# Complex power tables of a state-space mixer: from VectorE to GpSimd, with GpSimd's other instructions cut in half

## The chip, the core and the metric

One core of a Trainium2 chip runs the whole program. The metric is device time in microseconds. The engines are named as in the profile: PE is TensorE, DVE is VectorE, ACT is ScalarE, POOL is GpSimd, SP issues most transfers.

## The reference

The program computes a two-layer trunk over 512 tokens of width 1024 in float32. What matters here is the first half-step feed-forward and the state-space mixer (S5) behind it:

```python
x = x + 0.5 * swiglu(rms_norm(x, g[0]), ffn_w_in[l, 0], ffn_w_out[l, 0])
h = rms_norm(x, g[1])
# S5: 64 groups of 16 channels, 64 complex states each
lam_bar = jnp.exp(lam * step)                       # one complex number per state
b_bar = ((lam_bar - 1.0) / lam)[..., None] * b
# x_t = lam_bar x_{t-1} + b_bar u_t ;  y_t = Re(C x_t) + D u_t
```

The kernel computes the recurrence in 64 steps of 8 tokens. For that it needs powers of `lam_bar` times B and C (the block operators), and tables of the real and imaginary part of the phase after each of the 64 steps. Both depend on the weights alone, and they are made while the first feed-forward runs on PE.

## The kernel before

**The weights.** The feed-forward is computed to nearly float32 precision from packs of 128x1024 weights. SP loads pack n into one of four slots of `w_raw` (L475) once DVE has split pack n-4. ACT copies it rounded into `w_split` (L749) once PE has used up pack n-4, DVE subtracts to get the remainder (L1159, the DVE instruction `split`), and PE multiplies three times for each tile (L1590, L1591, L1592). One pack takes PE 24 matmuls.

**The first feed-forward** runs as two halves, `FFN0A1` (packs 0 to 32) and `FFN0A2` (33 to 65), each of 11 tiles of the inner dimension. The IN part has two packs a tile, and behind it the gate: DVE L1169, ACT L755, DVE L1171, ACT L757, DVE L1173 (`g_split`). The OUT part has 11 packs, for eight output tiles d = 0 to 7 of eleven products each; DVE adds each tile to the stream `x_res` (L1259, L1260). The first output tile needs all 11 gated tiles, the last one too.

**The block operators.** There are eight blocks of eight groups. `make_powers(k)` on POOL makes `CP` and `BP` with six TENSOR_TENSOR instructions (L569, L574, L576 of 1152 elements a partition; L579, L580, L582 of 1024), signals `s_made`, and stores part of `CP` with a transfer of its own. PE then turns block k (`turn_block`, L1663 and L1667) at a fixed place of its own order, written in `TURN_AT`: block 0 after IN tile 4, blocks 1 and 2 after IN tiles 7 and 9, blocks 3 and 4 after OUT tiles 2 and 5, blocks 5 to 7 after IN tiles 2, 5 and 8 of the second half. PE waits there for `s_made`. `make_powers(k)` in turn waits at L574 until PE has turned block k-1. ACT and DVE finish the block (`copy_ops`, `block_taps`) at the places in `TAPS_AT`, and SP stores it.

**The tables.** `block_tables(k)` on DVE (L1202 to L1208) makes the phase tables of block k: four products into `gate`, `up` and the two halves of a part of `OUTB`, and then a subtraction and an addition. The factors are `PA` and `PB`, where neighbouring powers of one group lie 64 elements apart; one factor of each product is repeated along the innermost dimension, and the other is read with steps of 64 elements. The places in `TABLES_AT` say after which tile DVE does so, and from the same places `table_stores` works out behind which weight pack SP waits for the tables (`s_phase`) and stores them. Block k's tables may overwrite `OUTB` once those of block k-1 are stored (`s_tabst`).

**POOL's order**: preparations, `make_powers(0)`, powers for `PB`, `make_powers(1)`, powers of `PB`, `make_powers(2)`, powers of `PA`, a memset that signals `s_near`, then `make_powers(3)` to `(7)`, then the loads of finished operators.

Of the kernel before, what the change touches and what calls it, by code (L numbers as in the profile page):

```python
# [28 lines left out]
ALU = mybir.AluOpType  # L29
# [3 lines left out]
P = 128  # L33
# [24 lines left out]
FFN0A1 = 0  # L58
FFN0A2 = FFN0A1 + 3 * HALF
# [14 lines left out]
TILES = {FFN0A1: HALF, FFN0A2: HALF, FFN0B: FT, FFN1A: FT, FFN1B: FT}  # L74
F_BASE = {FFN0A1: 0, FFN0A2: HALF, FFN0B: FT, FFN1A: 2 * FT, FFN1B: 3 * FT}
# [5 lines left out]
IN, OUT = range(2)  # L81
# [2 lines left out]
           (FFN0A2, IN, 2): 5, (FFN0A2, IN, 5): 6, (FFN0A2, IN, 8): 7}  # L84
TAPS_AT = {(FFN0A1, IN, 5): 0, (FFN0A1, IN, 8): 1, (FFN0A1, IN, 10): 2, (FFN0A1, OUT, 3): 3, (FFN0A1, OUT, 6): 4,
           (FFN0A2, IN, 3): 5, (FFN0A2, IN, 6): 6, (FFN0A2, IN, 9): 7}
TABLES_AT = {(FFN0A1, OUT, 0): 0, (FFN0A1, OUT, 1): 1, (FFN0A1, OUT, 4): 2, (FFN0A2, IN, 1): 3, (FFN0A2, IN, 4): 4,
             (FFN0A2, IN, 6): 5, (FFN0A2, IN, 8): 6, (FFN0A2, IN, 10): 7}

N_IN0A, N_S5, N_IN0B, N_KV, N_LAT, N_DQ, N_IN1B, N_FINAL = range(8)  # L90

# [14 lines left out]
O_B, O_COS, O_SIN, O_C, O_T = 0, 1024, 1536, 2048, 3072  # L106
# [3 lines left out]
def build(nc, xT, wstream, cols, consts, mask, pos, lam, bcd, dskip, out):  # L110
# [18 lines left out]
    GT = at("gate", [P, SEQ], F32, o_s + 2 * K)  # L129
    UT = at("up", [P, SEQ], F32, o_s + 4 * K)  # L130
# [27 lines left out]
    PW = tmp("lam_pow", [P, 2, M, GROUPS])  # L158
    PWS = tmp("lam_pow_signed", [P, 2, M, GROUPS])
    PA = tmp("u64_pow", [P, 2, 8, GROUPS])  # L160
    PB = tmp("u8_pow", [P, 2, 8, GROUPS])
    EC = tmp("e_coef", [P, 2, GROUPS])
    BC = [tmp("bc_in_even", [P, 4, GB * GC]), at("bc_in_odd", [P, 4, GB * GC], F32, o_s + 16 * K)]
    CP = tmp("c_pow", [P, GB, M, GC])
    BP = tmp("b_pow", [P, GB, T, GC])
    OUTB = tmp("ops_out", [P, 2048])
    DS = tmp("d_skip", [GC, GROUPS])
    DI = tmp("d_eye", [GC, GB, GC])
    TM = tmp("s5_tmp", [P, GB * M * GC])
# [39 lines left out]
    def sem(name):  # L209
        return nc.alloc_semaphore(name)  # L210
# [8 lines left out]
    s_tabst = sem("tables_stored")  # L219
# [15 lines left out]
    s_g_hi, s_g_lo = sem("g_hi"), sem("g_lo")  # L235
# [6 lines left out]
    s_cp = sem("c_and_b_steps")  # L242
    s_phase, s_window = sem("phase_steps"), sem("taps_in_window")
    s_small = sem("coefficients_ready")
    s_zero_taps = sem("taps_before_zero")
    s_near, s_sq0, s_sum0 = sem("table_powers_ready"), sem("first_squares"), sem("first_squares_added")
    s_ang, s_rope, s_pch = sem("rope_angles_reduced"), sem("rope_tables_ready"), sem("pool_step")

    s_made, s_turned, s_taps, s_btc = sem("powers_made"), sem("ops_turned"), sem("taps_ready"), sem("b_op_copied")
# [28 lines left out]
    def block_groups(k):  # L278

        return slice(k * GB, (k + 1) * GB)  # L280
# [132 lines left out]
    with nc.Block() as block:  # L413
# [115 lines left out]
        def _(pool):  # L529
# [8 lines left out]
            tt, ts = nc.gpsimd.tensor_tensor, nc.gpsimd.tensor_scalar  # L538
# [10 lines left out]
            def make_powers(k):  # L549

                first = k == 0

                def chan(ap):
                    return ap.rearrange("p (g c) -> p g c", g=GB)

                def power(tab, ri, n):
                    return (tab[:, ri, 0:n, block_groups(k)].rearrange("p m g -> p g m").unsqueeze(3)
                            .broadcast_to([P, GB, n, GC]))

                def spread(ap, n):  # L560
                    return chan(ap).unsqueeze(2).broadcast_to([P, GB, n, GC])

                tmc = TM[:].rearrange("p (g m c) -> p g m c", g=GB, m=M)
                tmb = TM[:, 0:GB * T * GC].rearrange("p (g m c) -> p g m c", g=GB, m=T)
                if k + 1 < BLOCKS:
                    pool.dma_start(BC[(k + 1) % 2][:], bcd[k + 1]).then_inc(s_bc[(k + 1) % 2], 16)
                bc = BC[k % 2]
                pool.wait_ge(s_bc[k % 2], 16 * (k // 2 + 1))
                tt(tmc, spread(bc[:, 3, :], M), power(PWS, 1, M), ALU.mult)  # L569
                if not first:  # L570

                    pool.wait_ge(s_turned, k)
                    pool.wait_ge(s_cpst, k * 16)
                tt(CP[:], spread(bc[:, 2, :], M), power(PWS, 0, M), ALU.mult).then_inc(s_cp, 1)  # L574
                pool.wait_ge(s_cp, k * 3 + 1)
                tt(CP[:], CP[:], tmc, ALU.subtract).then_inc(s_cp, 1)  # L576

                pool.wait_ge(s_cp, k * 3 + 2)
                tt(BP[:], spread(bc[:, 0, :], T), power(PW, 0, T), ALU.mult)  # L579
                tt(tmb, spread(bc[:, 1, :], T), power(PW, 1, T), ALU.mult).then_inc(s_cp, 1)  # L580
                pool.wait_ge(s_cp, k * 3 + 3)
                tt(BP[:], BP[:], tmb, ALU.subtract).then_inc(s_made, 1)  # L582
                pool.wait_ge(s_made, k + 1)
                pool.dma_start(ops_dram[k][:, O_C:O_T].rearrange("p (g n) -> p g n", g=GB),
                               CP[:, :, 1:M, :].rearrange("p g m c -> p g (m c)")).then_inc(s_cpst, 16)


            nc.gpsimd.memset(RSTD[:], 0.0).then_inc(s_warm, 1)
# [49 lines left out]
            make_powers(2)  # L638
            squared(tt, link, (PA[:, 0, 1, :], PA[:, 1, 1, :]), (PB[:, 0, 4, :], PB[:, 1, 4, :]), t1, t2)
            powers(tt, link, PA, 7, t1, t2)  # L640
            nc.gpsimd.memset(TM[:, 0:8], 0.0).then_inc(s_near, 1)
            pool.wait_ge(s_near, 1)
            for k in range(3, BLOCKS):
                make_powers(k)


            pool.wait_ge(s_opdma, 16 * OPS_STORES * BLOCKS)
# [492 lines left out]
        def _(dve):  # L1140
# [8 lines left out]
            tt, ts, stt = nc.vector.tensor_tensor, nc.vector.tensor_scalar, nc.vector.scalar_tensor_tensor  # L1149
# [34 lines left out]
                link(ts(dst[:], bank[:], 1.0 / width, EPS, ALU.mult, ALU.add))  # L1184
                nc.vector.reciprocal(dst[:], dst[:]).then_inc(s_rcp, 1)

            def block_tables(k, F):

                if k == 0:
                    dve.wait_ge(s_near, 1)  # L1190
                else:

                    dve.wait_ge(s_tabst, k * 16)
                dve.wait_ge(s_g_lo, F + 1)
                gs = block_groups(k)
                ar, ai = (PA[:, ri, :, gs].rearrange("p a g -> p g a").unsqueeze(3).broadcast_to([P, GB, 8, 8])
                          for ri in range(2))
                br, bi = (PB[:, ri, :, gs].rearrange("p b g -> p g b").unsqueeze(2).broadcast_to([P, GB, 8, 8])
                          for ri in range(2))
                ct, st, v1, v2 = (ap.rearrange("p (g a b) -> p g a b", g=GB, a=8) for ap in (  # L1200
                    OUTB[:, O_COS:O_COS + 512], OUTB[:, O_SIN:O_SIN + 512], GT[:], UT[:]))
                tt(v1, ai, bi, ALU.mult)  # L1202
                tt(v2, ar, bi, ALU.mult)
                tt(ct, ar, br, ALU.mult)
                tt(st, ai, br, ALU.mult).then_inc(s_phase, 1)
                dve.wait_ge(s_phase, k * 2 + 1)
                tt(ct, ct, v1, ALU.subtract)
                tt(st, st, v2, ALU.add).then_inc(s_phase, 1)  # L1208
                dve.wait_ge(s_phase, k * 2 + 2)

            def block_taps(k):

                link(tt(DI[:], DS[:, block_groups(k)].unsqueeze(2).broadcast_to([GC, GB, GC]),
# [901 lines left out]
```

## Time and profile before

| | |
|---|---|
| median of 3 runs | 1799.36 us (1798.47 to 1799.75) |
| the profiled execution: its own time | 1796.3 us |
| the profiled execution: its span | 1794.5 us |
| TensorE's mean granted clock | 0.997 |
| PE busy | 1773.4 us, 99% |
| DVE busy | 920.9 us, 51% |
| ACT busy | 646.2 us, 36% |
| POOL busy | 319.7 us, 18% |

The span goes from the first to the last instruction; the execution's own time is 1.8 us more. Busy shares are averages over the whole program: POOL is busy nearly all of its first 220 us, and hardly afterwards.

### The profile page before, as it was taken

How to read it: one execution, taken by the hardware profiler on the slowest of the kernel's cores; microseconds unless marked ns; L12 is line 12 of the kernel's file. 1: busy time of each engine (PE TensorE's matmuls, PEld its weight loads, DVE VectorE, ACT ScalarE, POOL GpSimd, SP SyncE). 2: the span in 40 equal slices, each digit the busy share in tenths (PEclk: the TensorE clock that was granted, in tenths of full speed). 3: DMA queues.
4: the chain of work that ended last, by engine and by line, in shares of the span. 5: the costliest groups of instructions: out<-in, count | busy, mean ns of one | idle time of the engine just before them, and what ended most of it. 6: DMA issues, size and time to landing. Idle time of an engine off the chain costs nothing.

```text
span 1794.5 us, 21493 instructions
## 1 busy us (share of the span) xinstructions
PE 1773.4 (99%) x8142; PEld 1453.2 (81%) x8142; DVE 920.9 (51%) x1059; ACT 646.2 (36%) x884; POOL 319.7 (18%) x274
## 2 busy tenths in 40 slices
PE   9999899999999999999999999999999999999998
PEld 6887788879888888888888888888866888888887
DVE  7768978647555444433374444333664554444333
ACT  6342233347434333322253333222454433333222
POOL 8997533016014000000000000000100200000000
PEclk9999999999999999999999999999999999999999
DMA  5353635588422222222223222222310322222221
GB/s 199 118 171 117 185 132 167 160 311 295 136 99 94 94 95 103 95 94 95 103 74 116 94 94 100 99 94 94 123 36 1 106 106 100 99 94 94 98 91 47
DMA packets 80977, 207.24 MB, mean 115 GB/s; under 512 B 24048, under 2 KB 34416, under 8 KB 79888
## 3 DMA queue, kind: packets, MB, share of 16 engines
q1 hardware_dynamic: 69664, 189.86, 31.4%
q0 software_dynamic: 2784, 14.29, 2.4%
q10 hardware_dynamic: 8464, 2.20, 0.5%
q8 instruction: 44, 0.72, 0.2%
q14 instruction: 21, 0.17, 0.0%
HBM read 183.25 MB, written 23.07 MB: 115 GB/s over the span
## 4 chain that ended last, share of the span: by engine, by line
PE 90%; DVE 4%; POOL 3%; issue 2%; ACT 1%; DMA 1%; SPq 0%; ACTq 0%; DVEq 0%; POOLq 0%
PE bank L1590 28%; PE bank L1592 27%; PE bank L1591 27%; PE bank L1920 1%; DVE w_split L1159 1%; PE bank L1901 1%; PE bank L1903 1%; PE bank L1768 1%; PE bank L1785 1%; PE bank L1778 1%; ACT w_split L749 0%; PE bank L1912 0%; DVE ops_out L1208 0%; PE bank L1620 0%; DMA x_res<-xT 0%
## 5 line engine op out<-in xcount | busy, mean ns | idle before, releaser
L1159 DVE TENSOR_TENSOR w_split<-w_raw,w_split 128x1024 fp32r<-128x1024 f32 x296 | 399.3, 1353 | 624.8 <-ACT w_split L749 624.1
L1590 PE MATMUL bank<-h_split,w_split 128*128 128x512 f32 x1504 | 589.5, 392 | 2.3 <-DVE gate L1171 0.8
L1592 PE MATMUL bank<-h_split,w_split 128*128 128x512 f32 x1504 | 585.7, 389 | 0.0
L1591 PE MATMUL bank<-h_split,w_split 128*128 128x512 f32 x1504 | 585.6, 389 | 0.0
L749 ACT ACTIVATE w_split<-w_raw 128x1024 fp32r<-128x1024 f32 x296 | 312.1, 1058 | 639.3 <-PE bank L1592 631.4
L1590 PE MATMUL bank<-g_split,w_split 128*128 128x512 f32 (+1 forms) x854 | 330.2, 387 | 8.1 <-DVE w_split L1159 5.0
L1590 PEld LDWEIGHTS bank<-h_split,w_split 128*128 128x128 f32 x1504 | 282.4, 188 | 64.7 <-DVE h_split L1178 1.9
L1591 PEld LDWEIGHTS bank<-h_split,w_split 128*128 128x128 f32 x1504 | 282.5, 188 | 59.3 <-issue 1.4
L1592 PEld LDWEIGHTS bank<-h_split,w_split 128*128 128x128 f32 x1504 | 282.4, 188 | 58.6
L1591 PE MATMUL bank<-g_split,w_split 128*128 128x512 f32 (+1 forms) x854 | 329.5, 386 | 0.0
L1592 PE MATMUL bank<-g_split,w_split 128*128 128x512 f32 (+1 forms) x854 | 329.4, 386 | 0.0
L547 POOL TENSOR_TENSOR sq_sum<-sq_sum,sq 128x512 f32<-128x512 f32 x39 | 51.1, 1310 | 1063.7 <-ACT sq L768 1063.7
L1590 PEld LDWEIGHTS bank<-g_split,w_split 128*128 128x128 f32 x854 | 161.6, 189 | 40.7 <-DVE w_split L1159 5.4
L1592 PEld LDWEIGHTS bank<-g_split,w_split 128*128 128x128 f32 x854 | 161.5, 189 | 32.1
L1591 PEld LDWEIGHTS bank<-g_split,w_split 128*128 128x128 f32 x854 | 161.6, 189 | 31.7
L755 ACT ACTIVATE gate<-gate 128x512 f32<-128x512 f32 x88 | 55.6, 632 | 203.8 <-DVE gate L1169 203.7
L1173 DVE TENSOR_TENSOR g_split<-gate,g_split 128x512 f32 (+1 forms) x88 | 76.9, 874 | 80.7 <-ACT g_split L757 80.7
L1171 DVE TENSOR_TENSOR gate<-gate,bank 128x512 f32<-128x512 f32 x88 | 60.6, 688 | 62.7 <-ACT gate L755 62.7
L757 ACT ACTIVATE g_split<-gate 128x512 f32 (+1 forms) x88 | 55.6, 632 | 72.7 <-DVE gate L1171 72.7
L1169 DVE TENSOR_TENSOR gate<-bank,rstd 128x512 f32<-128x512 f32 x88 | 60.1, 683 | 1.4 <-ACT rstd L786 1.4
L761 ACT ACTIVATE h_split<-x_res,cols 128x512 fp32r<-128x512 f32 x48 | 33.0, 717 | 51.8 <-DVE x_res L1260 48.2
L768 ACT ACTIVATE sq<-x_res 128x512 f32<-128x512 f32 x41 | 25.6, 623 | 50.3 <-DVE x_res L1260 38.2
(283 smaller groups left out, 1163.8 us busy)
## 6 DMA issues: line engine op xcount, KB each, us to landing
w_raw<-wstream SPq DMA_DIRECT2D x296, 512.0 KB, 3.5
op_slot<-s_ops SPq DMA_DIRECT2D x5, 2048.0 KB, 11.3
s_ops<-ops_out SPq DMA_DIRECT2D x16, 512.0 KB, 2.9
op_slot<-s_ops POOLq DMA_DIRECT2D x3, 2048.0 KB, 14.2
s_ops<-c_pow POOLq DMA_DIRECT2D x8, 512.0 KB, 4.6
s_ops<-k_window SPq DMA_DIRECT2D x64, 64.0 KB, 3.4
x_res<-xT SPq DMA_DIRECT2D x8, 256.0 KB, 6.5
s_u<-x_gained ACTq DMA_DIRECT2D x8, 256.0 KB, 6.9
```

What stands on the lines that cost most here:

```text
L547: nc.gpsimd.tensor_tensor(ACC[:], ACC[:], SQ[:, k % 2, :], ALU.add).then_inc(s_sum, 1)
L749: nc.scalar.activation(W[:, r, 0, :], RAW[:, r, :], ACT.Copy).then_inc(s_hi, 1)
L755: nc.scalar.activation(GT[:], GT[:], ACT.Silu).then_inc(s_silu, 1)
L757: nc.scalar.activation(gt_part(f, 0), GT[:], ACT.Copy).then_inc(s_g_hi, 1)
L761: nc.scalar.activation(dst[:, k, 0, :], X[:, k, :], ACT.Identity, scale=col(gains + k)).then_inc(s_h_hi, 1)
L1159: tt(W[:, r, 1, :], RAW[:, r, :], W[:, r, 0, :].bitcast(F32), ALU.subtract).then_inc(s_lo, 1)
L1169: tt(GT[:], gb[:], RSTD[:], ALU.mult).then_inc(s_gate, 1)
L1171: tt(GT[:], GT[:], ub[:], ALU.mult).then_inc(s_read, 1)
L1173: tt(gt_part(f, 1), GT[:], gt_part(f, 0).bitcast(F32), ALU.subtract).then_inc(s_g_lo, 1)
L1590: mm(bank, hi, x_hi, start=start, stop=True, skip_group_check=True)
L1591: mm(bank, hi, x_lo, start=False, stop=True, skip_group_check=True)
L1592: return mm(bank, lo, x_hi, start=False, stop=True, skip_group_check=True)
```

## The change

`make_powers` writes each of its six instructions as two, over groups 0 to 3 and 4 to 7 of the block. `block_tables` is deleted from DVE, and the same six instructions, not in halves, stand in POOL's `make_tables`, with `TM` (POOL's scratch) in place of `gate` and `up`. `make_tables(0)` stands ahead of `make_powers(3)`, and the others are set between the later powers. `TABLES_AT`, which now only places SP's stores, is partly moved: the stores of tables 0 to 7 stand behind packs 30, 34, 39, 45, 49, 53, 59 and 63; before, they stood behind 31, 32, 36, 45, 51, 55, 59 and 63. `TURN_AT` and `TAPS_AT` stay.

```diff
-TABLES_AT = {(FFN0A1, OUT, 0): 0, (FFN0A1, OUT, 1): 1, (FFN0A1, OUT, 4): 2, (FFN0A2, IN, 1): 3, (FFN0A2, IN, 4): 4,
-             (FFN0A2, IN, 6): 5, (FFN0A2, IN, 8): 6, (FFN0A2, IN, 10): 7}
+TABLES_AT = {(FFN0A1, IN, 10): 0, (FFN0A1, OUT, 2): 1, (FFN0A1, OUT, 6): 2, (FFN0A2, IN, 1): 3, (FFN0A2, IN, 3): 4,
+             (FFN0A2, IN, 5): 5, (FFN0A2, IN, 8): 6, (FFN0A2, IN, 10): 7}
...
+                def in_halves(dst, a, b, op):
+                    for gs in (slice(0, GB // 2), slice(GB // 2, GB)):
+                        ins = tt(dst[:, gs], a[:, gs], b[:, gs], op)
+                    return ins
...
-                tt(tmc, spread(bc[:, 3, :], M), power(PWS, 1, M), ALU.mult)
+                in_halves(tmc, spread(bc[:, 3, :], M), power(PWS, 1, M), ALU.mult)
...
+            def make_tables(k):
+                if k >= 1:
+                    pool.wait_ge(s_tabst, k * 16)
+                gs = block_groups(k)
+                ar, ai = (PA[:, ri, :, gs].rearrange("p a g -> p g a").unsqueeze(3).broadcast_to([P, GB, 8, 8])
+                          for ri in range(2))
+                br, bi = (PB[:, ri, :, gs].rearrange("p b g -> p g b").unsqueeze(2).broadcast_to([P, GB, 8, 8])
+                          for ri in range(2))
+                ct, st, v1, v2 = (ap.rearrange("p (g a b) -> p g a b", g=GB, a=8) for ap in (
+                    OUTB[:, O_COS:O_COS + 512], OUTB[:, O_SIN:O_SIN + 512], TM[:, 0:512], TM[:, 512:1024]))
+                tt(v1, ai, bi, ALU.mult)
+                tt(v2, ar, bi, ALU.mult)
+                tt(ct, ar, br, ALU.mult)
+                tt(st, ai, br, ALU.mult).then_inc(s_phase, 1)
+                pool.wait_ge(s_phase, k * 2 + 1)
+                tt(ct, ct, v1, ALU.subtract)
+                tt(st, st, v2, ALU.add).then_inc(s_phase, 1)
+                pool.wait_ge(s_phase, k * 2 + 2)
...
-            nc.gpsimd.memset(TM[:, 0:8], 0.0).then_inc(s_near, 1)
-            pool.wait_ge(s_near, 1)
-            for k in range(3, BLOCKS):
-                make_powers(k)
+            make_tables(0)
+            make_powers(3)
+            make_tables(1)
+            make_powers(4)
+            make_tables(2)
+            make_powers(5)
+            make_tables(3)
+            make_tables(4)
+            make_powers(6)
+            make_tables(5)
+            make_powers(7)
+            make_tables(6)
+            make_tables(7)
...
-            def block_tables(k, F):
...
-                if (stage, place, i) in TABLES_AT:
-                    block_tables(TABLES_AT[stage, place, i], F)
```

## Rows read from the trace of the kernel before

**Rows 1.** The page, part 1: busy time, share of the span, instructions.

```profile
PE 1773.4 (99%) x8142; PEld 1453.2 (81%) x8142; DVE 920.9 (51%) x1059; ACT 646.2 (36%) x884; POOL 319.7 (18%) x274
```

**Rows 2.** Waits of PE, 0 to 420 us: total us, times, longest us.

```profile
PE bank L1590 <- DVE w_split L1159: 5.0, 1, 5.0
PE bank L1590 <- DVE g_split L1173: 3.2, 1, 3.2
...
PE bank L1590 <- DVE gate L1171: 0.8, 1, 0.8
...
PE bank L1663 <- POOL b_pow L582: 0.5, 1, 0.5
```

**Rows 3.** Windows: busy by engine (instructions), granted clock, DMA share, GB/s.

```profile
148.00:149.00 1.00, 1.00 (x4) 0.81 (x3) 1.00 (x1) 0.00 (x0) 0.92 (x2) 0.50 0.00 0
...
196.00:355.00 159.00, 158.19 (x766) 130.00 (x759) 121.44 (x111) 52.32 (x75) 49.69 (x22) 1.00 0.51 153
```

**Rows 4.** Timeline of PE: start us, us, instruction, idle before it.

```profile
142.89 0.39 PE L1592 MATMUL bank<-g_split,w_split 128*128 128x512 f32 x1
146.44 0.50 PE L1590 MATMUL bank<-g_split,w_split 128*128 128x512 f32 x1 [3.16 <-DVE g_split L1173]
...
163.90 0.63 PE L1663 MATMUL bank<-c_pow,b_pow 128*16 128x128 f32 x16
...
186.18 0.79 PE L1590 MATMUL bank<-g_split,w_split 128*128 128x512 f32 x1 [4.95 <-DVE w_split L1159]
...
191.84 0.40 PE L1591 MATMUL bank<-g_split,w_split 128*128 128x512 f32 x1
...
195.80 0.63 PE L1663 MATMUL bank<-c_pow,b_pow 128*16 128x128 f32 x16
```

**Rows 5.** Timeline of DVE, 97 to 188 us.

```profile
97.03 1.28 DVE L1159 TENSOR_TENSOR w_split<-w_raw,w_split 128x1024 fp32r<-128x1024 f32 x1
...
143.89 2.50 DVE L1173 TENSOR_TENSOR g_split<-gate,g_split 128x512 fp32r<-128x512 f32 x1 [0.70 <-ACT g_split L757]
...
167.15 2.26 DVE L1202 TENSOR_TENSOR gate<-u_pow 128x512 f32<-128x512 f32 x1 [0.85 <-DMA s_ops<-ops_out]
...
182.15 5.11 DVE L1159 TENSOR_TENSOR w_split<-w_raw,w_split 128x1024 fp32r<-128x1024 f32 x2
```

**Rows 6.** Timeline of POOL.

```profile
63.83 2.40 POOL L582 TENSOR_TENSOR b_pow<-b_pow,s_tmp 128x1024 f32<-128x1024 f32 x1
...
97.30 1.32 POOL L376 TENSOR_TENSOR u_pow<-u_pow,s_tmp 128x128 f32<-128x128 f32 x1
...
133.95 0.59 POOL L377 TENSOR_TENSOR u_pow<-u_pow,s_tmp 128x192 f32<-128x192 f32 x1
...
148.34 3.25 POOL L582 TENSOR_TENSOR b_pow<-b_pow,s_tmp 128x1024 f32<-128x1024 f32 x1
...
246.75 2.30 POOL L574 TENSOR_TENSOR c_pow<-bc_in_even,lam_pow_signed 128x1152 f32<-128x1152 f32 x1 [30.14 <-PE bank L1667]
```

**Rows 7.** POOL by line: duration ns min/median/max, first and last start.

```profile
L569 POOL TENSOR_TENSOR s_tmp<-bc_in_odd,lam_pow_signed x4: 2252/2270/2275, 75.8 to 261.2; 128x1152 f32<-128x1152 f32 x4
...
L582 POOL TENSOR_TENSOR b_pow<-b_pow,s_tmp x8: 2396/2958/3262, 63.8 to 292.6; 128x1024 f32<-128x1024 f32 x8
...
L547 POOL TENSOR_TENSOR sq_sum<-sq_sum,sq x12: 1282/1294/1332, 361.0 to 544.2; 128x512 f32<-128x512 f32 x12
```

**Rows 8.** POOL's small instructions, grouped by form: busy us, mean ns.

```profile
L375 POOL TENSOR_TENSOR u_pow<-u_pow 128x192 f32<-128x192 f32 x2 | 1.2, 596 | 0.0
...
L375 POOL TENSOR_TENSOR u_pow<-u_pow 128x64 f32<-128x64 f32 x3 | 1.0, 317 | 0.0
```

**Rows 9.** DVE's table instructions by line: duration ns min/median/max.

```profile
L1203 DVE TENSOR_TENSOR up<-u_pow x8: 1103/1117/3610, 159.2 to 346.9; 128x512 f32<-128x512 f32 x8
...
L1208 DVE TENSOR_TENSOR ops_out<-ops_out,up x8: 677/686/3165, 163.0 to 350.8; 128x512 f32<-128x512 f32 x8
```

**Rows 10.** Waits of SP's queue, 0 to 420 us.

```profile
SPq L444 <- DVE ops_out L1208: 52.4, 7, 16.6
```

More of the change, by code:

```diff
@@ L245, in build @@
     s_zero_taps = sem("taps_before_zero")
-    s_near, s_sq0, s_sum0 = sem("table_powers_ready"), sem("first_squares"), sem("first_squares_added")
+    s_sq0, s_sum0 = sem("first_squares"), sem("first_squares_added")
     s_ang, s_rope, s_pch = sem("rope_angles_reduced"), sem("rope_tables_ready"), sem("pool_step")
@@ L573, in make_powers @@
                     pool.wait_ge(s_cpst, k * 16)
-                tt(CP[:], spread(bc[:, 2, :], M), power(PWS, 0, M), ALU.mult).then_inc(s_cp, 1)
+                in_halves(CP, spread(bc[:, 2, :], M), power(PWS, 0, M), ALU.mult).then_inc(s_cp, 1)
                 pool.wait_ge(s_cp, k * 3 + 1)
-                tt(CP[:], CP[:], tmc, ALU.subtract).then_inc(s_cp, 1)
+                in_halves(CP, CP, tmc, ALU.subtract).then_inc(s_cp, 1)
                 pool.wait_ge(s_cp, k * 3 + 2)
-                tt(BP[:], spread(bc[:, 0, :], T), power(PW, 0, T), ALU.mult)
-                tt(tmb, spread(bc[:, 1, :], T), power(PW, 1, T), ALU.mult).then_inc(s_cp, 1)
+                in_halves(BP, spread(bc[:, 0, :], T), power(PW, 0, T), ALU.mult)
+                in_halves(tmb, spread(bc[:, 1, :], T), power(PW, 1, T), ALU.mult).then_inc(s_cp, 1)
                 pool.wait_ge(s_cp, k * 3 + 3)
-                tt(BP[:], BP[:], tmb, ALU.subtract).then_inc(s_made, 1)
+                in_halves(BP, BP, tmb, ALU.subtract).then_inc(s_made, 1)
                 pool.wait_ge(s_made, k + 1)
@@ L1185, in mean_rcp @@
                 nc.vector.reciprocal(dst[:], dst[:]).then_inc(s_rcp, 1)
-            def block_tables(k, F):
[L1189 to L1209, printed above, removed]
             def block_taps(k):
@@ L1218, in s5_ops @@
             def s5_ops(stage, place, i):
-                F = F_BASE[stage] + (i if place == IN else TILES[stage] - 1)
                 if (stage, place, i) in TAPS_AT:
                     block_taps(TAPS_AT[stage, place, i])
-                if (stage, place, i) in TABLES_AT:
-                    block_tables(TABLES_AT[stage, place, i], F)
             def ffn_in_turn(stage, i):
```

## The prediction

> **What bounds the kernel now.** I read the page first: PE is busy 99% of the span [rows 1], so the kernel is one long line of matmuls and only what makes PE wait, or lowers its clock, can be won. The page says little about where that happens, so the second view is the table of PE's waits over the first 420 us, the part that the change touches. It has two waits that count, 5.0 us for a weight split on DVE and 3.2 us for a gated tile on DVE, and two small ones, 0.8 us and 0.5 us [rows 2]. Third, the timeline of PE places them: the first ends at 146.44, at the start of the OUT part; the second at 186.18 [rows 4]. Fourth, the windows: behind the first wait, at 148 us, the granted clock is 0.50, which is 1.2 GHz, while from 196 to 355 us it is 1.00, and PE is there busy 158.19 of 159 us [rows 3]. So each long wait is paid twice. A matmul at full clock is followed by the next after 0.227 us. The windows show the first fall from about 147.3 to 150.7, 3.4 us at half speed: 1.7 us lost. From 186.18 to 191.84 there are 13 matmuls, worth 2.95 us, in 5.66 us: 2.7 us lost [rows 4]. The sum to be had is 3.3 + 1.7 + 5.1 + 2.7 = 12.8 us, 0.7% of the time.
>
> Fifth, the timelines of DVE and POOL side by side say why DVE is late. POOL and DVE instructions that read two operands from SBUF don't overlap. The `g_split` at 143.89 takes 2.50 us, where its work is 0.69 us. The second set of tables occupies DVE from 167.15 to 182.15, 15 us, and the split that PE needs starts only then [rows 5]. Alone, a table product takes 1.10 us and a table sum 0.68 us [rows 9], so the set would be 5.8 us. The rest is waiting for POOL's instructions of 2.3 to 3 us. The other way round it costs POOL too: the DVE split at 97.03 (1.28 us, to 98.31) holds up a POOL instruction of 128 elements, which takes 1.32 instead of 0.46 us [rows 5, 6]. That is 0.87 us lost to POOL for each weight split, and in the same way some 0.46 us for each `g_split`.
>
> **The change part by part.** *Tables off DVE.* The second wait goes, with its clock loss: 7.8 us. DVE then has one split (1.2 us) and at times one sum in each pack of 5.44 us, so nothing on DVE is late next. *Halves.* DVE waits at most half as long for POOL. The `g_split` at 143.89 was due at 143.12, when PE ran out. Its chain had two such waits, of 2.3 and 1.8 us; in halves I count about half of each, leaving PE a wait of some 0.5 us and no fall of the clock: the 0.8 us and 0.5 us waits of rows 2 had none. That is 4.5 us. The 0.8 us wait at 292 us, behind a set of tables, goes too.
>
> So PE, left alone, would reach its turn of block 3 at 163.9 - 4.5 = 159.4 instead of 163.90, and that of block 4 24.1 us later (195.80 - 163.90 - 7.8). What waits there is POOL's work, so the sum is made on POOL.
>
> *What a half costs.* POOL's instructions of 64 and 192 elements take 317 and 596 ns [rows 8]: 2.2 ns an element and, less the 0.04 us by which neighbours overlap, a fixed 0.12 to 0.14 us. Six more instructions a block are 0.7 us. *What the DVE takes from it.* Undisturbed, a block is 0.6 (transfer issue) + 2 x 2.24 (L569's smallest) + 2.6 (L576, by L582's rate) + 2 x 2.0 (L579 and L580 at L569's rate) + 2.4 (L582's smallest) + 0.3 = 14.4 us [rows 7]. Block 0 took 16.7 us from 49.54 to 66.23, so 2.3 us went to DVE. In halves DVE is let in twice as often. Its work per pack is fixed by PE: a split a pack and a `g_split` every second one are 0.87 + 0.23 = 1.1 us in 5.44 us, which over block 0 is 3.4 us and more. So block 0 is ready 0.7 + 1.3 = 2.0 us later than 66.23, and PE, which already waits 0.5 us for it [rows 2], waits 2.5 us there. POOL has then block 1, block 2 and the small powers to do, and ends them before at 134.54 [rows 6]. Now it ends them at 134.54 + 3 x 0.7 + 2.0 = 138.6 us. The bounds of this: 136.6 if DVE takes no more than it does now, 139.5 if it takes all it can.
>
> *What a set of tables costs on POOL.* No POOL row has this reading. Lower bound: a product at the rate of L569, whose factors are also repeated, 2252 x 512 / 1152 = 1.0 us, and a sum like L547, 1.29 us: 4 x 1.0 + 2 x 1.29 = 6.6 us [rows 7]. Upper bound: L547's 1.29 us times the ratio that DVE shows between a product (1.10) and a sum (0.68): 2.09 us, and the set is 10.9 us [rows 7, 9]. I take the repeated form with the surcharge in us that DVE shows, 1.0 + 0.43 = 1.43 us: 4 x 1.43 + 2.58, 8.4 us with the gaps, because one factor is repeated and one is read in large steps. The Trainium skill (GPSIMD Engine Reference, Performance pitfalls for Q7 kernels) says that a GpSimd core that reads with steps of more than 8 bytes pays about half more for each element. By that rule a product at 1.29 us would become 1.94 us, the set 10.3 us, and the time 1805.3 us instead of 1801.5, an estimate; no row here shows such a reading on POOL.
>
> *The sum.* Set 0 stands ahead of block 3: 138.6 + 8.4 + 15.1 (a block in halves) + 5.0 (DVE's share over the 4.4 packs in which PE moves) = 167.1 us. PE arrives at 159.4 + 2.0 = 161.4 and waits 5.7 us: the new wait is as long as the one removed. Then 1.25 us for the transfer's issue, set 1 with 8.4, block 4 with 15.1, DVE's share 5.0: 196.9 us. PE arrives at 167.1 + 24.1 and 2 us of low clock = 193.2, waits 3.7 us, and turns block 4 at 197.0 instead of 195.80. Behind it the clock is low for about 1.7 us' worth, which this kernel did not have there. From then on POOL is ahead: block 5 is wanted at about 246 (POOL waits 30.14 us there now [rows 6]) and needs 197 + 1.3 + 8.4 + 20 = 227. The later sets go into such waits, and set 7 is stored at about 340, where it now is at 354. Sum: + 1.2 + 1.7 - 0.8 = + 2.1 us. The profiled execution has 1796.3 us; that is 1798.4 for it. The median of the runs lies 3.1 us above the profiled one, and carried to it this is 1801.5 us.
>
> *SP.* It waits for table 1 behind pack 34 until about 177. It waited 52.4 us for tables already, at most 16.6 us at once [rows 10], and PE had no wait for it: a load has some 12 us in hand. Store 0 moves behind pack 30 and its operator stores, lands at about 159, and set 1 starts after 168. Nothing for either. DVE's order loses 48 instructions, ACT's none.
>
> **The rivals.** (1) POOL keeps ahead: sets of 6.6 us, DVE's share as now (3.6 us a block with its set). Block 3 is ready at 136.6 + 6.6 + 15.1 + 3.6 = 161.9, a wait of 1.5 us, and block 4 at 188.4, a wait of 2.4 us. That is 7.4 + 0.8 = 8.2 us faster: 1791.2 us. For it: the repeated factor is cheap on POOL (L569). Against: all three terms must be at their lower bound. (2) The reading in large steps is dear on POOL as it is on DVE: 10.9 us a set, twice, is + 5.0, and DVE's full share another + 1: + 8 us, 1807.5 us. It decides from about 9.3 us a set on. For it: DVE's ratio of 1.6. Against: POOL spends 2.2 ns on an element anyway, where DVE spends half of that, and part of the reading may hide behind it. This is the one on the other side. The skill's rule on large steps, quoted above, speaks for this rival. (3) The stores in SP's queue hold up the weight packs, as soon as a set is later than the 12 us in hand: 5 us of wait and 2.7 us of clock more, 1809. Against: rows 10.
>
> **How the numbers follow.** Forecast 0.42, of which its own range is 1798 to 1805; rival 1 0.22; rival 2 0.28; rival 3 0.04; the rest, 0.04, is evenly spread. Bounds of no change are 0.2%, 3.6 us, about what a measurement of this kernel can tell. Faster: rival 1 and 0.02. Same: 0.34 of the forecast and 0.02. Slower: 0.08 of the forecast (block 3 late by another 2 us), rivals 2 and 3. The range goes from rival 1 to rival 2 with a little of what is beyond, 1791 to 1809.
>
> **What would show it.** In PE's waits the 5.0 and 3.2 us are gone; in their place stand waits of L1663 for POOL's `b_pow`: 2.5 us at about 68, 5 to 6 us at 162, 3 to 4 us at 193. POOL's set takes 8.4 us and 1.4 us a product; its halves of L569 take 1.2 us. If set 0 ends before 145 and no wait for `b_pow` is over 2 us, rival 1 holds. The forecast is wrong most easily in DVE's share of POOL's time, which enters five times, and in the product's price, which enters eight.

## The result and the profile after

The changed kernel has a median of 1801.51 us (1799.24 to 1803.3, 14 runs) beside 1797.91 us (1795.88 to 1799.75, 14 runs) for the kernel before on the same chip. The ratio is 1.0018, with a 95% interval of 1.0012 to 1.0025: 3.2 us slower by the ratio, 3.6 us by the medians, which is inside the 0.2% that the prediction calls no change, at its upper edge. The profiled execution has 1799.24 us, its span 1797.3 us; before it was 1796.3 and 1794.5. It is the fastest of the 14, 2.3 us below the median, so the waits below are not those of a typical one; the run changed_again has a second profile.

The page of the changed kernel, its first line and part 1, answers to [rows 1]:

```profile
span 1797.3 us, 21531 instructions
...
PE 1773.2 (99%) x8142; PEld 1454.1 (81%) x8142; DVE 868.4 (48%) x1011; ACT 646.8 (36%) x884; POOL 408.8 (23%) x369
```

DVE has 52 us less and POOL 89 us more. PE is busy as long as before and the span is 2.8 us longer, so the time must be in PE's waits. The waits of PE in the changed kernel, 0 to 420 us, answer to [rows 2]:

```profile
PE bank L1674 <- POOL b_pow L567: 10.1, 3, 3.9
PE bank L1601 <- DVE w_split L1316: 2.6, 2, 2.3
...
PE bank L1601 <- DVE g_split L1211: 0.7, 1, 0.7
PE bank L1601 <- DVE gate L1209: 0.2, 1, 0.2
```

The waits for DVE of [rows 2], 5.0, 3.2 and 0.8 us, are gone or small, and 10.1 us of waits for POOL's `b_pow` stand in their place. (The 2.3 us for L1316 is at 10 us, in a part that the change doesn't touch, and comes and goes with the execution.) PE's timeline of the changed kernel, with the idle time in brackets, places the three, and answers to [rows 4]:

```profile
69.36 1.05 PE L1674 MATMUL bank<-c_pow,b_pow 128*16 128x128 f32 x16 [2.35 <-POOL b_pow L567]
...
168.37 0.41 PE L1674 MATMUL bank<-c_pow,b_pow 128*16 128x128 f32 x4 [3.88 <-POOL b_pow L567]
...
197.81 0.28 PE L1674 MATMUL bank<-c_pow,b_pow 128*16 128x128 f32 x1 [3.89 <-POOL b_pow L567]
```

They are the turns of blocks 0, 3 and 4, the three places that the prediction named. The windows of the changed kernel (us, busy by engine, granted clock, DMA share, GB/s) answer to [rows 3]:

```profile
69.00:72.00 3.00, 2.64 (x25) 2.14 (x25) 2.30 (x3) 0.63 (x1) 2.60 (x7) 0.50 0.30 70
168.00:171.00 3.00, 2.63 (x25) 2.14 (x25) 0.00 (x0) 0.00 (x0) 2.68 (x4) 0.50 0.96 343
199.00:202.00 3.00, 3.00 (x11) 2.52 (x10) 0.00 (x0) 0.00 (x0) 2.98 (x4) 0.50 0.87 326
205.00:355.00 150.00, 150.00 (x712) 123.19 (x712) 93.69 (x75) 51.81 (x73) 110.59 (x73) 1.00 0.53 154
```

Behind each wait the granted clock is 0.50, 1.2 GHz. In finer windows it is low for 3.4 us each time, 1.7 us lost. The last row says where the change is good: from 205 to 355 us PE is busy all 150.00 us at 2.4 GHz, where it was 158.19 of 159 us before [rows 3]. The chain of waits, followed back from PE's turn at 197.81, is POOL without a gap from 34.81 us on, where the view begins: POOL is the bound from ahead of block 0 to block 4.

POOL's timeline of the changed kernel gives the dates (start, duration):

```profile
66.82 2.49 POOL L567 TENSOR_TENSOR b_pow<-b_pow,s_tmp 128x512 f32<-128x512 f32 x2
...
138.58 1.46 POOL L607 TENSOR_TENSOR s_tmp<-u_pow 128x512 f32<-128x512 f32 x1
...
164.85 3.46 POOL L567 TENSOR_TENSOR b_pow<-b_pow,s_tmp 128x512 f32<-128x512 f32 x2
...
194.42 3.34 POOL L567 TENSOR_TENSOR b_pow<-b_pow,s_tmp 128x512 f32<-128x512 f32 x2
```

Block 0 is ready at 69.3, set 0 begins at 138.58, block 3 is ready at 168.3 and block 4 at 197.8. The last product (L610) and the last sum (L613) of a set by line (min/median/max ns), which answer to [rows 9]:

```profile
L610 POOL TENSOR_TENSOR ops_out<-u_pow x8: 1454/1483/2464, 142.8 to 341.4; 128x512 f32<-128x512 f32 x8
...
L613 POOL TENSOR_TENSOR ops_out<-ops_out,s_tmp x8: 1282/1291/1302, 146.6 to 345.1; 128x512 f32<-128x512 f32 x8
```

SP's waits for tables, 52.4 us in [rows 10], are 3.6 us.

### The profile page after: what moved, and what is told of

Same layout as the page of the kernel before. It is cut to its first block, busy times and chain, and to the rows that moved or that the text cites. A ratio compares the mean times of both kernels' runs of the same rounds, so it can differ in the third digit from the quotient of the medians.

```text
span 1797.3 us, 21531 instructions
## 1 busy us (share of the span) xinstructions
PE 1773.2 (99%) x8142; PEld 1454.1 (81%) x8142; DVE 868.4 (48%) x1011; ACT 646.8 (36%) x884; POOL 408.8 (23%) x369
## 4 chain that ended last, share of the span: by engine, by line
PE 88%; POOL 10%; DVE 1%; issue 1%; ACT 1%; DMA 0%; SPq 0%; ACTq 0%; DVEq 0%; POOLq 0%
PE bank L1601 27%; PE bank L1602 27%; PE bank L1603 27%; POOL c_pow L567 2%; POOL s_tmp L567 2%; POOL b_pow L567 2%; PE bank L1931 1%; PE bank L1912 1%; PE bank L1914 1%; PE bank L1779 1%; PE bank L1796 1%; PE bank L1789 1%; POOL s_tmp L373 1%; POOL s_tmp L374 0%; PE bank L1923 0%
## 5 line engine op out<-in xcount | busy, mean ns | idle before, releaser
L1197 DVE TENSOR_TENSOR w_split<-w_raw,w_split 128x1024 fp32r<-128x1024 f32 x296 | 407.7, 1380 | 678.8 <-ACT w_split L787 678.4
L1211 DVE TENSOR_TENSOR g_split<-gate,g_split 128x512 f32 (+1 forms) x88 | 70.3, 799 | 80.7 <-ACT g_split L795 80.7
L1209 DVE TENSOR_TENSOR gate<-gate,bank 128x512 f32<-128x512 f32 x88 | 60.6, 688 | 62.6 <-ACT gate L793 62.6
```

Source lines behind the costliest of these rows:

```text
L1197: tt(W[:, r, 1, :], RAW[:, r, :], W[:, r, 0, :].bitcast(F32), ALU.subtract).then_inc(s_lo, 1)
L1209: tt(GT[:], GT[:], ub[:], ALU.mult).then_inc(s_read, 1)
L1211: tt(gt_part(f, 1), GT[:], gt_part(f, 0).bitcast(F32), ALU.subtract).then_inc(s_g_lo, 1)
```

## The experiments

Each series has its own runs of the kernel before, on the same chip: medians of 1796.48 us (series 1, 34 runs), 1796.10 us (series 2, 21), 1796.13 us (series 3, 22) and 1795.89 us (series 4, 9). All ratios are to these, with 95% intervals. The theory was the one of the prediction: PE waits for POOL because the sets stand ahead of blocks 3 and 4, and the halves take from POOL what they give to DVE. The main rivals were that the price of the sets decides, or what the halves do to PE's early waits. Each run lists the waits of one profiled execution, and its time is the median of all: in block0_whole, small_steps, powers_first_whole, powers_first_halves3 and spread_all_halves the profiled one lies 1.1 to 2.8 us above that median.

### Series 1: the two parts apart, and the order

**halves_alone**: the kernel before, with the halves at all powers; the tables stay on DVE.

```diff
+for gs in (slice(0, GB // 2), slice(GB // 2, GB)):
+    ins = tt(dst[:, gs], a[:, gs], b[:, gs], op)
```

> The kernel before with POOL's powers in halves and nothing else changed; the tables stay on DVE at their old places. Theory (POOL's blocks set PE's turns): block 0 is ready 2 to 3 us later, so PE waits about 2.4 us there and its clock falls for 3.4 us (1.7 us lost): +4. The wait of 3.2 us for g_split at the start of the OUT part shrinks to under 1 us with no fall of the clock: -4.5. The second set of tables on DVE takes some 11 instead of 15 us, so the split behind it is late by 1 us or less instead of 5: -6. Sum 4 to 8 us faster than before, near 1792 us. Rival (halves only cost POOL time and DVE gains nothing): the 5.0 us wait stays and the time is 2 to 4 us above before.

Measured: 1795.71 us, 0.9994 (0.9986 to 1.0003). Its waits of PE:

```profile
PE bank L1669 <- POOL b_pow L566: 5.2, 1, 5.2
PE bank L1596 <- DVE w_split L1165: 3.8, 3, 1.7
...
PE bank L1596 <- DVE g_split L1179: 1.1, 1, 1.1
```

A miss: 4 to 8 us were expected. The waits for DVE shrink as hoped (3.2 to 1.1 us, 5.0 to three of at most 1.7 us). But block 0 is ready at 71.1, 4.9 us later than at 66.2, and the wait of 5.2 us with 3.4 us of low clock behind it gives nearly all back. Of the 4.9 us the halves made 2.8: in this execution POOL began the block 2.1 us later too (51.63 instead of 49.54).

**tables_whole**: the changed kernel, with whole instructions.

```diff
-for gs in (slice(0, GB // 2), slice(GB // 2, GB)):
+for gs in (slice(0, GB),):
```

> The changed kernel with POOL's powers whole again; the tables stay on POOL and in the changed order. Theory: block 0 is back at 66 to 67 us with a wait of 0.5 us for it and no fall of the clock; set 0 begins at about 135 and takes 8.2 us; block 3 is ready at 160 to 161, where PE arrives at about 160; block 4 is ready at about 187, PE waits about 3 us. Sum about 6 to 8 us faster than before, 1790 to 1792 us. Rival (the tables on POOL cost the time, not the halves): waits for b_pow of 3 to 4 us at blocks 3 and 4 as in the changed kernel, and a time within 1 us of it.

Measured: 1799.09 us, 1.0012 (1.0003 to 1.002). A miss: slower instead of 6 to 8 us faster. By the ratios it is 1.1 us below the changed kernel, about what the rival had. The wait at block 3 is 0.64 us, but there is one of 9.39 us at block 4, with 10.2 us of low clock around it. POOL's timeline of this kernel shows half of the reason:

```profile
166.89 1.46 POOL L607 TENSOR_TENSOR s_tmp<-u_pow 128x512 f32<-128x512 f32 x1 [4.51 <-DMA s_ops<-ops_out]
```

POOL is done with block 3 at 161.1, and set 1 may not start, since set 0 is still in the buffer: SP issues its store at 160.74 only, behind the operator stores of block 2 (155.32 to 160.7). That is 4.5 of the 7.6 us by which block 4 is later than expected (194.65 instead of 187); in most of the rest, set 1 takes 10.8 us, disturbed by DVE, instead of 8.2. The store takes part as soon as POOL is fast; in the changed kernel POOL is late enough to hide it.

**powers_first_whole**: blocks 3 and 4 ahead of the sets, one set between, and the stores moved with them.

```diff
-order: T0 P3 T1 P4 T2 P5 T3 T4 P6 T5 P7 T6 T7, in halves
+order: P3 T0 P4 T1 T2 P5 T3 T4 P6 T5 P7 T6 T7, whole
-TABLES_AT = {(FFN0A1, IN, 10): 0, (FFN0A1, OUT, 2): 1, (FFN0A1, OUT, 6): 2, ...
+TABLES_AT = {(FFN0A1, OUT, 2): 0, (FFN0A1, OUT, 5): 1, (FFN0A1, OUT, 7): 2, ...
```

> The changed kernel with whole powers, and with POOL's order turned: block 3 ahead of set 0, block 4 ahead of set 1, and the stores of sets 0 to 2 at later places of SP's order. Theory: no wait of PE for b_pow but the 0.5 us at block 0. The wait of 3.2 us for g_split at the start of the OUT part comes back, with its fall of the clock (5 us), since block 3 runs there in whole instructions. Against before only the second wait (7.8 us) and the 0.8 us one are gone: 8 to 9 us faster, about 1789 us. Rival (POOL's total work counts, not its order): as the changed kernel.

Measured: 1793.76 us, 0.9983 (0.9975 to 0.9992), 2.7 us faster where 8 to 9 were expected. The waits at blocks 3 and 4 are gone. What remains: 2.21 us at block 0 with a fall of the clock, 1.54 us for ACT's operator copies at block 2, 1.94 us for a `g_split`, 2.00 us at 244.14 for the gate's product (DVE L1209) with another fall, 0.93 us at block 6.

**powers_first_halves3**: the same, with blocks 3 to 7 in halves.

```diff
-for gs in (slice(0, GB),):
+for gs in (slice(0, GB // 2), slice(GB // 2, GB)) if k >= 3 else (slice(0, GB),):
```

> As the kernel with the turned order, but with blocks 3 to 7 in halves and blocks 0 to 2 whole. Theory: the halves now stand only where PE doesn't wait for POOL, and the wait for g_split falls under 1 us without a fall of the clock: 12 to 13 us faster than before, about 1785 us. Rival (halves give nothing at g_split): equal to the kernel with the turned order and whole powers.

Measured: 1792.82 us, 0.9977 (0.9968 to 0.9986), 3.7 us faster where 12 to 13 were expected. The `g_split` wait falls to 0.65 us and the one at 244 is gone; one of 4.84 us, with 6.8 us of low clock, stands at block 6 (0.93 us in the run before). This execution is the slowest of the 11, 2.8 us above their median, so the others need not have it in this size. POOL's waits in this kernel, 200 to 300 us:

```profile
POOL s_tmp L607 <- DMA s_ops<-ops_out: 10.1, 2, 6.7
```

Two sets stand together there (T3, T4), and block 6 behind them: the second waits 3.39 us at 247.60 for the first to be stored. The order still puts work that PE awaits behind work that it doesn't.

### Series 2: block 0, the large steps, and a version without these faults

**block0_whole**: the changed kernel, with block 0 whole (`if k > 0` beside the halves).

> The changed kernel with block 0 alone whole again (blocks 1 to 7 in halves, sets on POOL, the changed order). Theory (POOL's chain up to block 4 sets the time): the wait at block 0 falls from 2.4 to 0.5 to 2.2 us, but what PE wins there it gives back at blocks 3 and 4, since POOL only gets the 0.7 us of split instructions and about 1 us of DVE's share back: block 4 at 195 to 196 us, time 1 to 2 us below the changed kernel (1799 to 1800 us by the median of the first series). Rival (the wait at block 0 with its fall of the clock is paid in full): 4 us below the changed kernel.

Measured: 1798.81 us, 1.0016 (1.0007 to 1.0025). The wait at block 0 is 0.55 us, but at block 3 it is 7.64 us and at block 4 3.81 us, 12.9 us in all with 0.86 us at block 2. What PE wins at block 0 it loses at block 3, where POOL sets the date: as the theory has it. The gain is smaller than the 1 to 2 us expected, since POOL has lost its lead again by block 4, which is ready at 198.1 and not at 195 to 196.

**small_steps**: the changed kernel, where the products read their second factor from neighbouring elements instead of in large steps. The tables then don't hold the phases.

```diff
-br, bi = (PB[:, ri, :, gs].rearrange("p b g -> p g b").unsqueeze(2)
+br, bi = (PB[:, ri].rearrange("p b g -> p (b g)")[:, 0:GB * 8].rearrange("p (g b) -> p g b", g=GB).unsqueeze(2)
```

> The changed kernel, with one part of the computation changed: POOL's four products of a set read their second factor from neighbouring elements of PB instead of elements 64 apart, so the tables don't hold the phases; everything else is the same, instruction for instruction. If the large steps have a price of their own, as the prediction took it, a product falls from 1.46 us to 1.05 to 1.1 us, a set from 8.1 to 6.5 us, block 3 is ready 1.6 us and block 4 3.2 us earlier, and the time falls by about 3 us. Rival (the price is that of any product with a repeated factor of 8 elements): a product stays at 1.46 us and the time too.

Measured: 1797.71 us, 1.0007 (0.9998 to 1.0016). The last product of this kernel, whose line number is one higher here:

```profile
L611 POOL TENSOR_TENSOR ops_out<-u_pow x8: 1154/1168/1623, 143.6 to 336.7; 128x512 f32<-128x512 f32 x8
```

The large steps cost 0.30 us of 1.46 us a product, 1.2 us a set: their price is shown. By the ratios the kernel is 2 us below the changed one, but the intervals of the two overlap. The waits for `b_pow` are 5.16, 3.45 and 3.40 us in its profiled execution, where block 0 was late (ready at 70.9), and blocks 3 and 4 are turned at 168.7 and 197.9, not earlier than in the changed kernel.

**dve_tables_halves3**: the kernel before, with only blocks 3 to 7 in halves and the tables on DVE; the guard `if k >= 3` as above.

> The kernel before, tables on DVE at their old places, with only blocks 3 to 7 in halves. Theory: block 0 is as before (wait 0.5 to 2.2 us), the 3.2 us wait for g_split falls to about 1 us, the 5.0 us wait behind set 1 to about 1 us as in the kernel with halves alone, and up to 3 us of short waits for weight splits stay in the second half: about 7 us faster than before, 1789 to 1790 us. Rival (halves alone had gained nothing because of DVE, not because of block 0): equal to halves alone, 1795 to 1796 us.

Measured: 1789.29 us (1788.9 to 1790.2, 5 runs), 0.9962 (0.9949 to 0.9976). As expected: halves are worth 6.8 us without a single table moved, if block 0 is left whole. What is left are three waits for weight splits, 3.7 us together, and 1.6 us for a `g_split`.

**sets_spread**: powers_first_halves3, with every set behind a block that PE awaits and no two sets together while a block is due soon.

```diff
-order: P3 T0 P4 T1 T2 P5 T3 T4 P6 T5 P7 T6 T7
+order: P3 T0 P4 T1 T2 P5 T3 P6 T4 P7 T5 T6 T7
-TABLES_AT = {..., (FFN0A2, IN, 1): 3, (FFN0A2, IN, 3): 4, (FFN0A2, IN, 5): 5, ...
+TABLES_AT = {..., (FFN0A2, IN, 1): 3, (FFN0A2, IN, 4): 4, (FFN0A2, IN, 7): 5, ...
```

> As the kernel with the turned order and blocks 3 to 7 in halves, and set 4 moved behind block 6 and set 5 behind block 7, with their stores later, so that no block waits behind two sets. Theory: the 4.8 us wait for block 6 and its fall of the clock, seen in one execution, go; no wait for b_pow remains but the one at block 0; 3 to 7 us below that execution, and by the medians 0 to 3 us below that kernel, 1790 to 1793 us. Rival (set 4 later holds up a store and with it SP's weight packs): a new wait for a weight split at 270 to 320 us, and no gain.

Measured: 1785.17 us (1785.01 to 1785.59, 5 runs), 0.9938 (0.9924 to 0.9952): 10.9 us below the kernel before, and more than the 1790 to 1793 us that were expected. By the ratios it is 7.0 us below powers_first_halves3. Its waits of PE, 0 to 420 us:

```profile
PE bank L1601 <- DVE g_split L1211: 1.8, 2, 1.5
PE bank L1601 <- DVE w_split L1316: 1.6, 1, 1.6
...
PE bank L1674 <- POOL b_pow L567: 0.5, 1, 0.5
```

Up to the end of this part the granted clock does not fall once. It is 4.1 us below dve_tables_halves3, which has the same halves, the tables on DVE and was measured beside it; no run of one reaches those of the other. So moving the tables to POOL is right; the changed kernel placed them wrongly.

### Series 3: what the halves are worth once the order is right

**spread_all_halves**: sets_spread, with all blocks in halves (no guard).

> The kernel with the sets spread out (the fastest so far, 1785.2 us), but with all eight blocks in halves instead of 3 to 7. Theory: nothing later absorbs the wait at block 0 here, so it is paid in full: block 0 is ready 3 to 5 us later, the clock falls behind it (1.7 us), and the time is 4 to 7 us above 1785. Rival (splitting block 0 costs no more than its 0.7 us, and the longer waits for it seen so far were scatter): within 1.5 us of 1785.

Measured: 1790.21 us, 0.9964 (0.9952 to 0.9977), 5.0 us more than sets_spread by the medians, 4.7 by the ratios. Blocks 1 and 2 are in halves here too, but no wait stands at them. Its waits have one new row, at block 0, with the clock low from 69.0 to 75.8:

```profile
PE bank L1674 <- POOL b_pow L567: 5.1, 1, 5.1
```

**spread_whole**: sets_spread, with no block in halves.

> The same kernel with no block in halves. If the halves are what shortens the wait at the start of the OUT part, it comes back at 3.2 us with a fall of the clock (1.7 us), and the time is 3 to 5 us above 1785. Rival (with the tables off DVE the whole instructions do as well): within 1.5 us of 1785.

Measured: 1795.6 us, 0.9996 (0.9987 to 1.0005), 10.4 us more than sets_spread where 3 to 5 were expected. Its waits:

```profile
PE bank L1601 <- DVE gate L1209: 5.8, 3, 3.5
PE bank L1601 <- DVE g_split L1211: 3.2, 2, 3.0
```

The longest of the `gate` waits, 3.49 us, ends at 301.19. DVE's timeline of this kernel there:

```profile
289.33 9.82 DVE L1197 TENSOR_TENSOR w_split<-w_raw,w_split 128x1024 fp32r<-128x1024 f32 x2
```

and POOL's:

```profile
289.15 0.93 POOL L591 DMA_DIRECT2D s_ops<-c_pow  x1 [0.30 <-POOL b_pow L567]
290.10 1.48 POOL L607 TENSOR_TENSOR s_tmp<-u_pow 128x512 f32<-128x512 f32 x1
291.52 1.47 POOL L608 TENSOR_TENSOR s_tmp<-u_pow 128x512 f32<-128x512 f32 x1
292.95 1.46 POOL L609 TENSOR_TENSOR ops_out<-u_pow 128x512 f32<-128x512 f32 x1
294.38 1.46 POOL L610 TENSOR_TENSOR ops_out<-u_pow 128x512 f32<-128x512 f32 x1
295.92 2.15 POOL L612 TENSOR_TENSOR ops_out<-ops_out,s_tmp 128x512 f32<-128x512 f32 x1
```

Two splits whose work is 2.4 us take 9.82 us, of which the first takes 7.59, while four products of POOL each run at their undisturbed 1.46 us: none let DVE in. The sum at L612, before which POOL waits for its own products, is the first that takes longer (2.15 instead of 1.29 us). That gave a new theory: DVE gets in where POOL waits for a semaphore, not reliably between instructions that follow one another.

**changed_again**: the changed kernel, unchanged.

> The changed kernel itself, on one chip with the two others. The first series gave 1.0018 of before. By the theory it is 14 to 17 us above the kernel with the sets spread out, with waits for b_pow at blocks 0, 3 and 4 of 8 to 14 us together in its profile and low clock behind at least two of them.

Measured: 1800.02 us, 1.002 (1.0011 to 1.0029). The waits for `b_pow` are 3.91 us at 69.61, 3.90 at 168.75 and 3.72 at 198.17. The wait at block 0, 2.35 us in the first profile, is 3.91 us here. The time is 14.9 us above sets_spread and the waits are 11.5 us together, with low clock behind each: as expected.

### Series 4: the new theory

**spread_whole_waits**: spread_whole, with a wait of POOL behind each of the first three products of a set. No instruction is cut.

```diff
-tt(v1, ai, bi, ALU.mult)
-tt(v2, ar, bi, ALU.mult)
-tt(ct, ar, br, ALU.mult)
+link(tt(v1, ai, bi, ALU.mult))
+link(tt(v2, ar, bi, ALU.mult))
+link(tt(ct, ar, br, ALU.mult))
```

> The kernel with the sets spread out and whole powers (1795.6 us, 10 us above its twin with blocks 3 to 7 in halves), with one edit: POOL waits for each of the first three products of a set before it starts the next. In its trace a weight split of DVE took 7.6 us, from 289.33 to 296.92, while POOL ran four products one behind the other, each in its undisturbed 1.46 us. If DVE isn't let in between POOL instructions that follow without a wait, the waits open three more gaps a set: no split takes more than some 3.5 us beside a set, PE's waits for the gate at 240 us (2.0 us) and 301 us (3.5 us, with a fall of the clock) go, and the time falls by 5 to 8 us, to 1788 to 1791. A set takes 0.2 us more alone. Rival (what counts is the length of the single instruction, and the whole powers cause the 10 us): products are held up nowhere new and the time stays within 1.5 us of 1795.6.

Measured: 1789.47 us, 0.9965 (0.9951 to 0.9979): 6.1 us less than spread_whole (each against 1796.13 or 1795.89 us before). The same place in POOL's timeline of this kernel:

```profile
292.77 1.47 POOL L608 TENSOR_TENSOR s_tmp<-u_pow 128x512 f32<-128x512 f32 x1
294.32 1.80 POOL L609 TENSOR_TENSOR ops_out<-u_pow 128x512 f32<-128x512 f32 x1
296.20 2.35 POOL L610 TENSOR_TENSOR ops_out<-u_pow 128x512 f32<-128x512 f32 x1
```

and DVE's:

```profile
293.74 1.06 DVE L1211 TENSOR_TENSOR g_split<-gate,g_split 128x512 fp32r<-128x512 f32 x1 [0.70 <-ACT g_split L795]
294.72 2.49 DVE L1197 TENSOR_TENSOR w_split<-w_raw,w_split 128x1024 fp32r<-128x1024 f32 x1
```

Now the products take turns with DVE (1.80 and 2.35 us), and from 200 to 355 us the longest split takes 3.70 us instead of 7.59. The `gate` waits are gone. A `g_split` wait of 2.99 us at 147.92, beside the powers and with low clock behind it, and 2.2 us at block 0 remain.

The traces bear the theory out beyond this place. In all 14 together, 53 weight splits of the first 360 us take over 3.8 us. In each of them the last 1.2 us, which is what a split alone takes, begin where POOL comes to a semaphore wait. In spread_whole two of them are beside sets, in spread_whole_waits none. Such a split costs time only where PE has nothing in hand: sets_spread, the fastest kernel, has four of them, of 5.6 to 7.6 us.

## Why the prediction was right in its total, and where its steps failed

The way to the time held: two waits for DVE go, three for POOL come, and the sum is about nothing. That 1801.5 us was forecast and 1801.51 measured is luck. The forecast is + 2.1 us on a median of 1799.36 us from 3 runs of the kernel before. Over 14 runs this median is 1797.91, 1.45 us lower, and the change adds 3.6 us (3.2 by the ratio), 1.5 us more.

- **Tables off DVE**, -7.8 us: the wait at 186 us is gone, and that at 292 us.
- **Halves**, -4.5 us: right in size, for another reason. PE's wait for `g_split` at the start of the OUT part is 0.74 us (expected 0.5), with no fall of the clock. But POOL runs set 0 beside it here (138.6 to 147.9), which is not in halves, where the kernel before runs block 3. In tables_whole, with no halves at all, the wait is 1.28 us and the clock doesn't fall either. So most of this term came from the order, and about 0.5 us from the halves.
- **Set 0's start**, 138.6 us: 138.58, which is in part luck: the 2.0 us in this sum hold the 0.7 us of block 0's split instructions, which 3 x 0.7 counts again, and POOL began block 0 0.7 us later than before. **The product**, 1.43 us: 1.46; the set of 8.4 us takes 9.3 us (set 0, to 147.9, with 1.0 us of DVE's share) and 8.3 us (set 1, undisturbed). **A block in halves with DVE's share**, 15.1 + 5.0 = 20.1 us: 20.1 (block 3) and 19.5 (block 4), from the issue of its transfer.
- **Block 3**, ready at 167.1: 168.3. The wait is 3.88 us instead of 5.7, since PE comes at 164.5 and not at 161.4. Of these 3.1 us, 1.7 are the low clock behind block 0, which the sum left out; 1.2 us PE was late already when it came to block 0 (67.0 us; before 65.8), most likely by the 2.3 us wait at the start of this execution, behind which the clock is low for 3.4 us.
- **Block 4**, turned at 197.0 with 3.7 us of wait: 197.81 and 3.89, and the clock falls behind it as said. Of the 1.2 us by which block 3 was late, 0.8 are left. The profiled execution has 1799.24 us instead of 1798.4, the same 0.8 us more.
- **Behind block 4** POOL is ahead, PE has no wait: right, 150.00 of 150 us. The last set is stored only at about 356 us, as before, not at 340: set 7 waits 8.56 us for the store of set 6, and POOL's loads of the finished operators wait 9.89 us for the store of set 7. It costs nothing: PE has no wait from 205 to 420 us.
- **Rival 1** (POOL keeps ahead) is out: set 0 ends at 147.9. **Rival 3** is out: SP's waits for tables fell to 3.6 us.
- **Rival 2** had the direction: large steps cost something, but not the set of 10.9 us. Without the large steps a product takes 1.17 us, with them 1.46: 25% more. The Trainium skill (GPSIMD Engine Reference, Performance pitfalls for Q7 kernels) has half more for an element read in large steps. Here one of the two factors is read so; where the rule and the measurement differ, the measurement decides. From the rule the prediction estimated a product of 1.94 us and a time of 1805.3 us.

Three steps failed, though the sum did not show it, because their errors lay where something else set the date.

*"In halves, DVE waits at most half as long for POOL"* fails. The size of POOL's instruction is not all that DVE waits for. In the changed kernel a split starts at 148.40, while POOL still issues a transfer, and takes 6.30 us, beside four halves of 128x576 elements of which none is disturbed. DVE's timeline of the changed kernel:

```profile
148.40 6.30 DVE L1197 TENSOR_TENSOR w_split<-w_raw,w_split 128x1024 fp32r<-128x1024 f32 x1
```

and POOL's:

```profile
148.85 2.42 POOL L567 TENSOR_TENSOR s_tmp<-bc_in_odd,lam_pow_signed 128x576 f32<-128x576 f32 x2
151.21 2.40 POOL L567 TENSOR_TENSOR c_pow<-bc_in_odd,lam_pow_signed 128x576 f32<-128x576 f32 x2
153.69 3.74 POOL L567 TENSOR_TENSOR c_pow<-c_pow,s_tmp 128x576 f32<-128x576 f32 x2
```

Its work of 1.2 us ends at 154.70, so it got in at about 153.5, at POOL's wait ahead of 153.69. At the same place in tables_whole, beside whole instructions, DVE's timeline has nearly the same:

```profile
144.47 6.05 DVE L1197 TENSOR_TENSOR w_split<-w_raw,w_split 128x1024 fp32r<-128x1024 f32 x1
```

Halves helped as a whole (dve_tables_halves3, -6.8 us), so cuts do let DVE in at times; series 4 shows that waits do it where instructions alone didn't. What decides between two halves without a wait was not found.

*"Block 0 is ready 2.0 us later"* is mis-sized. From the issue of its first transfer the block takes 16.5 to 16.7 us in all nine profiles in which it is whole, and 19.1 to 20.1 us in the five in which it is in halves: 2.4 to 3.4 us more. In halves it is ready at 69.3 to 71.1 us, 3.1 to 4.9 us later than before; the rest of that is POOL's start of the block, which lies between 49.5 and 51.6 us from one execution to the next, whole or in halves. And the wait has a fall of the clock behind it, which the sum left out. In a right order the halves of blocks 0 to 2 cost 5.0 us (spread_all_halves), with one wait, at block 0. In the changed kernel it is worth less: by the ratios (1.0018 and 1.002 beside block0_whole's 1.0016) 0.4 to 0.7 us, within the intervals nothing, because POOL is the bound at block 3 anyhow.

*"Nothing for either"*, said of SP, is right for this kernel only because POOL is late: the prediction had 9 us between the landing of store 0 at 159 and the start of set 1 at 168, and an earlier POOL uses them up. In tables_whole the store of set 0 costs POOL 4.51 us, and in powers_first_halves3 that of set 3 costs 3.39 us. Two misses of series 1 come in part from this edge.

Where did the expected gain go? Of the 12.8 us that the prediction counted as to be had, sets_spread gets 10.9, so they were there for the same parts in another order. They are not the sum of two independent parts. Blocks 3 to 7 in halves alone are worth 6.8 us (dve_tables_halves3, 0.9962). The tables on POOL in the good order, with whole powers, are worth nothing clear of noise (spread_whole, 0.9996): the wait at 186 us is gone, but POOL's sets now hold DVE up, and 5.8 us of waits for the gate stand in its place. Both together give 10.9 us. So the 7.8 us that the prediction gave to the tables alone show only if something lets DVE in. Between the changed kernel (1.0018 and 1.002) and sets_spread (0.9938) lie some 14.5 us. Of these, 5.0 us are the halves of blocks 0 to 2. The rest, 9.5 us, is the order, with the store places that belong to it; no run parts these two. The two waits of 3.9 us and their low clock in the changed kernel are of that size, 7.8 + 2 x 1.7 = 11.2 us.

## What to carry to other kernels

When work moves to the idle engine, it is its place in that engine's order that decides: first what the bound engine awaits, then the optional work, and no two pieces together that share a buffer if the store between them is slow. Where two engines hold each other up, let the other one in by waits in a long run of instructions, or by cutting them, but only in runs for which the bound engine doesn't wait itself. A sum that comes out right doesn't prove its terms: three of this one's were wrong in size or reason, and only kernels with another order, or with one part alone, showed it.

## What the hardware showed that was not expected

- DVE can be held over several POOL instructions, not only one: 9.82 us for two splits of 2.4 us of work, through four undisturbed products, and 6.30 us for a split of 1.2 us. Three waits more in each set took 6.1 us off the kernel, though they give POOL work between its instructions.
- The length of a wait alone doesn't say whether the clock falls. It fell behind waits of 2.35, 3.49 and 3.88 us. Behind waits of 2.00 and 2.21 us it fell in powers_first_whole, and not behind one of 2.00 us in spread_whole and of 2.21 us in spread_whole_waits. Behind a `g_split` wait of 2.99 us it fell in spread_whole_waits, and behind one of the same 2.99 us in spread_whole it did not. In these windows of spread_whole the first row is behind its 3.49 us wait; the second begins 0.3 us ahead of the end of its 2.99 us wait, at 146.31, and has the full 2.4 GHz:

```profile
301.70:304.70 3.00, 3.00 (x8) 2.33 (x8) 2.39 (x4) 2.94 (x8) 0.00 (x0) 0.50 0.12 48
146.00:149.30 3.30, 2.99 (x13) 2.49 (x14) 3.30 (x3) 0.00 (x0) 3.22 (x2) 1.00 0.00 0
```

- The same instructions up to block 0 gave a wait there of 0.5 us (tables_whole, sets_spread, spread_whole) or 2.2 us (powers_first_whole, powers_first_halves3, spread_whole_waits). Block 0 itself takes 16.5 to 16.7 us in all of them. In the three with 2.2 us POOL begins it at 51.3 to 51.5 us, in the others at 49.6 to 50.1, and what makes POOL late ahead of it was not found. So a wait of 2 us in one profile is no evidence by itself.
